# One MoE layer on one core: w2 of the last two expert pairs by column groups in turns, and both pairs' combinations of a group added up in one PSUM bank

## What is computed

```python
h = layer_norm(DEEPNORM_ALPHA * h + mix, ln1_g, ln1_b)
# router: top-1 group of 8, then top-2 of its 4 experts, gates add up to 1
for e in range(32):            # tokens gathered into slots of expert e
    hb = silu(xb @ w1[e]) * (xb @ w3[e])      # w1, w3: 2048 x 512
    y[tokens of e] += gate * (hb @ w2[e])     # w2: 512 x 2048
out = layer_norm(DEEPNORM_ALPHA * h + y, ln2_g, ln2_b)
```

## Time and profile before

| what | us |
|---|---|
| median of 3 runs | 1279.6 |
| lowest and highest | 1278.81 and 1279.9 |
| the profiled execution, its own time | 1281.4 |
| its span, first to last instruction | 1279.6 |
| TensorE busy, share of the span | 1235.5 (97%) |
| VectorE busy | 445.1 (35%) |
| bytes moved, mean rate | 472.28 MB, 369 GB/s |

### The profile page before, as it was taken

One profiled execution on the slowest core, in us unless ns is written; L12 is line 12 of the kernel. 1 busy time (PEld: TensorE's weight loads), 2 busy tenths in 40 slices (PEclk: granted clock), 3 DMA queues, 4 the chain that ended last, 5 costly groups with the idle time before them and its releaser, 6 DMA issues.

```text
span 1279.6 us, 15326 instructions
## 1 busy us (share of the span) xinstructions
PE 1235.5 (97%) x6669; PEld 709.6 (55%) x6669; DVE 445.1 (35%) x635; ACT 319.4 (25%) x545; POOL 7.7 (1%) x17
## 2 busy tenths in 40 slices
PE   6999999999999999999999989899899999989997
PEld 6989989988744444444443444444344444434433
DVE  7889996855310203133130202111010211111026
ACT  5443333533421211111111111111112111111212
POOL 1000000000000000000000000000000000000000
PEclk9999999999999999999999999999999999999998
DMA  9655555696999999999999999999999999999995
GB/s 311 208 187 196 167 195 173 233 370 245 351 393 422 413 411 428 427 426 427 429 431 432 430 430 431 431 430 427 435 425 429 428 426 429 427 427 427 424 406 228
DMA packets 67000, 472.28 MB, mean 369 GB/s; under 512 B 7291, under 2 KB 7875, under 8 KB 41075
## 3 DMA queue, kind: packets, MB, share of 16 engines
q1 hardware_dynamic: 66498, 470.47, 90.4%
q10 hardware_dynamic: 432, 0.79, 0.2%
HBM read 469.14 MB, written 2.10 MB: 368 GB/s over the span
## 4 chain that ended last, share of the span: by engine, by line
PE 82%; DMA 16%; DVE 1%; SPq 0%; issue 0%; ACT 0%; DVEq 0%
PE psum L958 34%; DMA places<-in_w_dram 15%; PE psum L706 9%; PE psum L733 9%; PE psum L1003 8%; PE psum L880 7%; PE psum L662 5%; PE psum L916 2%; PE psum L665 2%; PE psum L917 2%; PE psum L1038 1%; PE psum L945 1%; DMA places<-in_ln_in_b_dram 1%; PE psum L853 1%; DVE area_b L2035 0%; PE psum L627 0%
## 5 line engine op out<-in xcount | busy, mean ns | idle before, releaser
L958 PE MATMUL psum<-places,area_c 128*64 128x512 f32 x2048 | 458.2, 600 | 20.1 <-DMA places<-in_w_dram 20.1
L958 PEld LDWEIGHTS psum<-places,area_c 128*64 128x64 f32 x2048 | 146.6, 138 | 302.7 <-issue 298.4
L1003 PE MATMUL psum<-places,area_d 128*64 128x512 f32 x928 | 204.3, 598 | 2.2 <-DMA places<-in_w_dram 2.2
L1332 ACT ACTIVATE area_c<-psum,gain 128x128 f32<-128x128 f32 x256 | 96.5, 457 | 293.7 <-PE psum L880 293.7
L1905 DVE TENSOR_TENSOR area_a<-area_a,psum 128x512 f32<-128x512 f32 x56 | 38.3, 684 | 355.5 <-PE psum L917 355.5
L1499 DVE TENSOR_TENSOR w_low<-places,w_high 128x2048 fp32r<-128x2048 f32 x55 | 126.0, 2290 | 62.2 <-ACT w_high L1169 62.1
L1169 ACT ACTIVATE w_high<-places 128x2048 fp32r<-128x2048 f32 x55 | 105.4, 1916 | 143.8 <-PE psum L665 42.5
L1003 PEld LDWEIGHTS psum<-places,area_d 128*64 128x64 f32 x928 | 66.3, 138 | 129.5 <-issue 127.4
L880 PE MATMUL psum<-one_hot,area_b 128*128 128x128 f32 x1024 | 124.9, 278 | 0.3 <-DVE one_hot L1831 0.3
L880 PEld LDWEIGHTS psum<-one_hot,area_b 128*128 128x128 f32 x1024 | 118.0, 192 | 12.9 <-issue 12.2
L1889 DVE TENSOR_TENSOR y_low<-psum,y_high 128x512 fp32r<-128x512 f32 x64 | 42.7, 687 | 233.6 <-ACT y_high L1341 233.6
(11 more groups left out here) (220 smaller groups left out, 763.1 us busy)
## 6 DMA issues: line engine op xcount, KB each, us to landing
places<-in_w_dram SPq DMA_DIRECT2D x97, 2048.0 KB, 23.5
places<-in_w_dram SPq DMA_DIRECT2D x27, 4096.0 KB, 21.4
places<-in_w_dram SPq DMA_DIRECT2D x70, 1024.0 KB, 9.7
places<-in_w_in_dram SPq DMA_DIRECT2D x40, 1024.0 KB, 5.1
places<-in_w_out_dram SPq DMA_DIRECT2D x16, 1024.0 KB, 6.5
places<-in_w_dram SPq DMA_DIRECT2D x8, 512.0 KB, 18.5
places<-in_w_dram SPq DMA_DIRECT2D x16, 256.0 KB, 9.3
area_a<-in_x_dram SPq DMA_DIRECT2D x4, 512.0 KB, 6.0
```

The costliest lines, as they stand in the source:

```text
L958: mm = pe.matmul(psum[i * CAP:(i + 1) * CAP, j // UNITS, :], gathered[:, kk, i * CAP:(i + 1) * CAP], w[i][:, k, :], start=kk == 0, stop=kk ...
L1003: mm = pe.matmul(psum[i * CAP:(i + 1) * CAP, 4 + c, :], hidden_t[:, f, i * CAP:(i + 1) * CAP], w[i][:, c, :], start=f == 0, stop=f == FT - 1)
L1332: ins = act.activation(gathered[:, k, :], psum[:, 2 + g % 2, k % 4 * P:(k % 4 + 1) * P], ACT.Identity, scale=gain[:, 0, k:k + 1], bias=gai ...
```

## The change

In steps 14 and 15 the order of the work becomes: w1, w3 of step 14, the turn, w1, w3 of step 15, then w2 of both steps by column groups in turns: step 14 left (c = 0, 1), step 15 left, step 14 right (c = 2, 3), step 15 third (c = 2), step 15 fourth (c = 3). All these products are `column_products(s, f, c, ...)` (s = 0 for step 14, 1 for step 15). Step 14 writes PSUM banks 4 and 5, step 15 banks 6 and 7. There are eight results n = 0 to 7 in the order 14 c0, 14 c1, 15 c0, 15 c1, 14 c2, 14 c3, 15 c2, 15 c3, and eight combinations `combine_last(n)`: that of step 14 starts the bank pair of its group, that of step 15 adds on top, and VectorE adds the sum of both once (`add_last`). The identity matmuls that bring `area_a` into the last group's banks stand in `combine_last(5)`, ahead of the fourth products.

The loads follow: 176 to 183 are w1 and w3 of step 15 as whole halves; 184 and 185 are w2 left of step 14, 186 and 187 left of step 15, 188 and 189 right of step 14 (24 pieces of 512 KB in all), 190 and 191 third and fourth of step 15 (16 pieces of 256 KB). Quarters are used for loads 168 to 171 instead of 182 to 187. From load 132 on, two loads are issued together when the later one of their two slots is free. The rows of the last LayerNorm go to a slot that nothing else uses by then, and wait for nothing.

```diff
@@ last_two_steps, on TensorE
-                unit_products(b, b % TWO, lambda j: arrived(start + 2 * UNITS + j), False, units=range(UNITS))
+                for j in range(2 * UNITS):
+                    unit_products(b, b % TWO, lambda j: arrived(start + 2 * UNITS + j), False, units=(j,))
+                    if j == UNITS:
+                        pe.wait_ge(silu_ready, PAIRS)
...
                 for f in range(FT):
-                    hidden_rows(f, arrived(start + 3 * UNITS + f))
...
+                    for c in range(2):
+                        column_products(0, f, c, [half[:, f, c, :] for half in left], s_left)
+                    if f == FT // 2 - 1:
...
+                        pe.wait_ge(half_hidden, 1)
+                        pe.wait_ge(gt_drained, PAIRS)
...
                 pe.wait_ge(half_kept, 1)
...
+                pe.wait_ge(ht_drained, PAIRS)
+                pe.wait_ge(y_drained, NC * a)
                 for f in range(FT):
...
+                        column_products(1, f, c, [half[:, f, c, :] for half in last_left], s_last_left)
+                    if f < 2:
+                        combine_last(f)
+                pe.wait_ge(y_drained, LAST_Y + 2)
                 for f in range(FT):
...
+                    for c in range(2, NC):
+                        column_products(0, f, c, [half[:, f, c - 2, :] for half in right], s_right)
+                    if f < 2:
+                        combine_last(2 + f)
+                pe.wait_ge(y_drained, LAST_Y + 4)
+                for f in range(FT):
+                    column_products(1, f, 2, [third[:, i, f, :] for i in range(2)], s_third)
+                    if f % 2 == 1:
+                        combine_last(4 + f // 2)
+                for f in range(FT):
+                    column_products(1, f, 3, [fourth[:, i, f, :] for i in range(2)], s_tail)
                     if f == 1:
...
+                        combine_last(6)
+                combine_last(7)
@@ combine_last
+                if s == 0 and c >= 1:
+                    pe.wait_ge(comb_added, LAST_Y + (2 * (c - 1) if c > 1 else 0))
+                if s == 0 and last:
...
                         pe.matmul(psum[:, 2 + t, :], ident[:], area_a[:, t, LAST_COLS], start=True, stop=False)
...
+                    pe.matmul(psum[:, bank, :], by[:, t, :], y_high[:, n % 2, :],
+                              start=s == 0 and not last, stop=False)
+                    mm = pe.matmul(psum[:, bank, :], by[:, t, :], y_low[:, n % 2, :], start=False, stop=s == 1)
@@ the DMA queue
-            for m in range(WHOLE.stop, LAST):
-                load_half(m)
+            for m in range(WHOLE.stop, BY_COLUMNS, 2):
+                unit_used((m + 1 - PLACES) // STEP_UNITS, (m + 1 - PLACES) % STEP_UNITS)
+                if m in (LATE, LATE + 2):
+                    load_pair(m, m - LATE, PAIRS - 2)
...
-            sp.wait_ge(y_ready, NC * (PAIRS - 1))
...
+            last_unit_used(SLOTS - 2)
```

More of the change, by code:

```diff
@@ L918, in combine, with combine_last @@
                 mm.then_inc(comb_ready, 1)
[L920 to L925, removed]
+            def combine_last(n):
+                s, c = n // 2 % 2, n // 4 * 2 + n % 2
                 last = c == NC - 1
-                if last:
+                if s == 0 and c >= 1:
+                    pe.wait_ge(comb_added, LAST_Y + (2 * (c - 1) if c > 1 else 0))
+                if s == 0 and last:
                     for t in range(TT):
                         pe.matmul(psum[:, 2 + t, :], ident[:], area_a[:, t, LAST_COLS], start=True, stop=False)
-                pe.wait_ge(y_drained, NC * it + c + 1)
+                pe.wait_ge(y_drained, LAST_Y + n + 1)
+                by = (one_hot_t, one_hot_t_2)[s]
                 for t in range(TT):
                     bank = 2 * (c % 2) + t
-                    pe.matmul(psum[:, bank, :], one_hot_t_2[:, t, :], y_high[:, c % 2, :], start=not last, stop=False)
-                    mm = pe.matmul(psum[:, bank, :], one_hot_t_2[:, t, :], y_low[:, c % 2, :], start=False, stop=True)
-                    if last and t == 0:
+                    pe.matmul(psum[:, bank, :], by[:, t, :], y_high[:, n % 2, :],
+                              start=s == 0 and not last, stop=False)
+                    mm = pe.matmul(psum[:, bank, :], by[:, t, :], y_low[:, n % 2, :], start=False, stop=s == 1)
+                    if s == 1 and last and t == 0:
                         mm.then_inc(tile0_combined, 1)
@@ L1061, in last_two_steps @@
[L1061 to L1072, removed]
@@ new lines, in pair_of @@
+                def pair_of(m, form, **parts):
+                    return [slots[slot_of(BY_COLUMNS + m + i)].rearrange(form, **parts) for i in range(2)]
+                left, last_left, right = (pair_of(2 * j, "p (f c d) -> p f c d", f=FT, c=2) for j in range(3))
+                third, fourth = pair_of(6, "p (i f d) -> p i f d", i=2, f=FT)
+                for f in range(FT):
+                    for c in range(2):
[3 more added lines that the diff above has]
+                        pe.wait_ge(gt_drained, PAIRS)
+                        for h in range(FT // 2):
+                            mm = pe.transpose(psum[:, 0, h * P:(h + 1) * P], hidden[:, h * P:(h + 1) * P], ident[:])
+                        mm.then_inc(half_turned, 1)
+                        pe.wait_ge(hidden_ready, PAIRS)
+                        for h in range(FT // 2):
+                            at = (FT // 2 + h) * P
+                            mm = pe.transpose(psum[:, 1, h * P:(h + 1) * P], hidden[:, at:at + P], ident[:])
+                        mm.then_inc(ht_ready, 1)
@@ L1087, in last_two_steps @@
                     for c in range(2):
-                        last_rows(f, c, [wide[i][:, f, c, :] for i in range(2)], s_wide)
-                pe.wait_ge(y_drained, NC * b)
+                        column_products(1, f, c, [half[:, f, c, :] for half in last_left], s_last_left)
+                    if f < 2:
+                        combine_last(f)
+                pe.wait_ge(y_drained, LAST_Y + 2)
                 for f in range(FT):
-                    last_rows(f, 2, [narrow[0][:, i, f, :] for i in range(2)], s_third)
-                    if f == 1:
-                        combine_apart(b, 0)
@@ L1395, in last_step @@
                                ACT.Copy).then_inc(ht_drained, 1)
-                for c in range(NC):
-                    keep_y_high(it, c, True)
+                for n in range(2 * NC):
+                    keep_y_high(it - 1, n)
             act.wait_ge(s_gain, 16 * 2)
```

141 lines of the change are left out of this document (56 added, 85 removed).

## The result

The changed kernel takes a median of 1281.84 us (1280.47 to 1285.29, 20 runs), the kernel before 1280.07 us (1278.81 to 1281.86, 20 runs). The ratio is 1.0014, with a 95% interval of 1.0008 to 1.002. That is 1.8 us more, less than the 2.56 us that the prediction's bound of 0.2% allows: no change by that bound, but a small slowing that is clear of the noise, since the interval leaves out 1, and close to the 1281.3 us forecast. The profiled execution took 1282.77 us, with a span of 1281.0 us against 1279.6 before.

The account below looks back on a forecast made before the run. The weight stream bounds the kernel up to 1219.6 us, TensorE from there on. Last product + 2.05, tail - 0.4, so + 1.65 us on the median of 1279.6: 1281.3 forecast, small terms leaving 1280.3 to 1282.4, full range 1279.0 to 1284.0.

Parts of the forecast that it names:

- Landing of load 183: Last half of step 15's w3 lands at 1219.55 us, 0.15 of it added for more loads in quarters.
- the cover named in the prediction: Even loads 132 to 167 issue some 10 us later; two to three loads still queued, so cost nothing.
- Idle time: TensorE idles about 2 us, from 1217.5 to 1219.6, ahead of the last w3 pair.
- TensorE's work from there: From 1219.6 to the last product TensorE has 45.9 us of work, ending at 1265.5.
- Identity matmuls as the main loss: Now ahead of the last product, they make 1.9 of its 2.05 us delay.
- Data in time: After load 183, w2 pieces land at least 1.1 us before use; 2.55 us per 512 KB pair, 1.31 per 256 KB.
- Tail: From last product to tile 0's first statistics: 2.0 us against 2.42 before, 0.4 won.
- Sum: Last product 2.05 us later less 0.4 in the tail: 1.65 us more on the span.
- The clock falls: Rival: the idle time before the last w3 pair drops TensorE's clock, price 1.7 us, 1283.0; chance 0.20.
- Slow pieces: Rival: w2 pieces at 374 GB/s land the last right group row 2.0 us late, 1283.3; chance 0.10.
- TensorE keeps up: Rival: TensorE 4 us quicker than summed, so the end follows the last weight piece, 1277.3; chance 0.07.
- No wait at load 183: Rival: the stream runs 2 us ahead, so TensorE goes on at 1217.5, 1279.3; chance 0.07.

Follow-up runs that it names:

- e1: Changed kernel with the two identity matmuls put back behind the last product: median 1280.82 us, ratio 1.0006 to the kernel before.
- e4: Changed kernel with the identity matmuls done twice in their new place, the second overwriting the first: 1284.09 us, ratio 1.0032 to the kernel before.
- e5: Changed kernel without loading the fourth column group (2 MB); its products read the third group's weights: 1282.56 us, ratio 1.0018 to the kernel before.
- e8: Changed kernel with four unused 128x256 matmuls (1.9 us) in TensorE's idle place ahead of the last w3 pair: 1282.92 us, ratio 1.0024.
- e8b: Same kernel as e8, run again beside the unaltered changed kernel (c1): 1282.57 us, ratio 1.0017 to the kernel before.
- e9: Changed kernel with nine unused matmuls (4.1 us) in the idle place ahead of the last w3 pair: 1284.75 us, ratio 1.0035.
- c1: The changed kernel unaltered, as control: 1281.85 us, ratio 1.0015 to the kernel before.
- e2: Changed kernel with loads 180 to 183 cut into quarters instead of 168 to 171: 1281.37 us, ratio 1.0007 to the kernel before.
- e6: Kernel before with only its identity matmuls moved ahead of the third group's combination: 1281.61 us, ratio 1.0012.
- e3: Changed kernel with the edits of e1 and e2 together: 1280.3 us, ratio 1.0003 to the kernel before.
- e7: e3 with combinations 2 and 3, and 4 and 5, side by side: 1280.31 us, ratio 0.9999 to the kernel before.

## Why the prediction was right

Point by point, by its own steps.

- **Landing of load 183.** Forecast 1219.55, measured 1218.96, 0.6 us early. In the seven other profiles that leave these loads as they are (e1, e4, e5, e8, e8b, e9, c1) it landed between 1216.74 and 1218.99, so how near one execution comes is partly luck, and a term as small as the 0.15 for more quarters can't be seen. The later issues of the even loads cost nothing that shows: the DMA share is 1.00 to 1.01 at 426 to 427 GB/s from 960 to 1210, as the cover named in the prediction wanted.
- **Idle time.** Forecast about 2 us, measured 1.86, 2.04, 1.80 and 1.86 in the changed kernel, e1, e5 and c1, and 1.21 in e4. The mechanism was right, and e2 shows that it is the landing of the last halves that makes it. The term was sized from one profiled execution; in the median execution it may be nearer to 1 us (e8b, e9), which the noise leaves open.
- **TensorE's work from there.** Forecast 45.9 us, measured 45.94, and term by term no further off than 0.15 us: the w3 pair took 7.09 instead of 6.98 and the transposes of `hidden` 0.59 instead of 0.45, while the two row groups ahead of them took 3.43 instead of 3.58. With the earlier landing the last product ends at 1265.04 instead of 1265.5.
- **Identity matmuls as the main loss.** 1.9 of the 2.05 us. Removed (e1), doubled (e4) and added alone (e6), they moved the median by - 1.0, + 2.25 and + 1.5 us. In the two profiles the last product moved by 1.60 us (1263.44 to 1265.04), less than the 1.91 us of these matmuls, so the rest of the new order is even or slightly better there. Of the few tenths that combinations standing singly were to add no run speaks by itself; e1 without them has a ratio of 1.0006 (0.9997 to 1.0015), not told apart from the kernel before.
- **Data in time.** Forecast twelve pairs of 2.55 us; measured (1249.66 - 1218.96) / 12 = 2.56. The last weights landed at 1261.5 instead of 1260.6: here the step was 0.9 us short, since eight pairs took 11.85 us, 1.48 each instead of 1.31. The first six kept to 1.31 (the sixth landed at 1247.9 + 9.6 = 1257.5); the last two took 4.0 us together. The last pair's four records start near 1264.1, half-way through the last eight, so 2.6 us were left, and the miss stayed without effect.
- **Tail.** Forecast 2.0 us, measured 2.17: 1.40 us until y_low is done and read, where 1.35 had been set, and 0.74 for the two matmuls instead of 0.66, since the first took 0.50 behind an idle time.
- **Sum.** + 1.65 us forecast; on the span it was + 1.4 (1281.0), in the medians + 1.8. Two small errors of the trace steps, the landing (0.6 early) and the tail (0.17 long), are opposite in sign. That the median fell within 0.6 us of the forecast says no more than that: the medians' own difference is known to some 0.8 us.

One reading of the kernel before was slightly off: its chain doesn't stay on TensorE all the way from 1239.2, but spends 0.39 us on a copy by ScalarE (L1392) at 1245.21. Nothing in the forecast hangs on it.

The rivals. *The clock falls* did not come to pass: no granted clock of 0.50 between 1219 and 1265 in any of the profiles. But its condition, an idle time somewhat over 2.0 us, was wrong: the last section has a fall behind 1.95 us and none behind 3.05 us. That the clock stayed up behind 1.86 us is therefore not explained by the length of the idle time, and the prediction was in part lucky there. *Slow pieces*: no wait on a piece in the changed kernel. The Trainium skill's page "DMA: Bandwidth & Descriptors", section Bandwidth, measures 341 GB/s for a DMA of 1 MB and less for smaller ones. The trace disagrees as it did before: 403 GB/s over the 30.8 us of the 24 pieces of 512 KB, a pair of 1.05 MB each 2.56 us, and no wait. *TensorE keeps up* is false here, since TensorE waited for no piece and finished 3.5 us behind the last weights (1265.04 against 1261.5); in e3, the nearest to it, this was 1.7 us (1261.28 against 1259.6). *No wait at load 183* is false in both profiles of the changed kernel; whether the wait is shorter in the median execution stays open.

## What to carry to other kernels

Work that doesn't depend on the last data can be cheapest behind the last product, when the copying that follows leaves its engine idle there anyway: 1.9 us of matmuls cost 0.25 us in that place, and 1.7 us ahead of the last product (e1, e4). Before an order is refined to follow a stream more finely, see which of the two is bound at that point: from load 183 on 45.9 us of TensorE's work stood against 42.5 us of loads, and e5 took 2 MB of them away for no gain. A gap in front of a late load was 1.2 to 2.0 us long in five profiles of this study, so one profile doesn't size it; filling it with work of two lengths, with enough runs, does so better.

## What the runs showed of the hardware

- The length of an idle time doesn't tell whether TensorE's clock falls behind it. The first three rows below stand at the same place of the program, the first pair of w3 units of step 14. In the changed kernel TensorE stood idle for 2.07 us, and the granted clock fell to 0.50, the 1.2 GHz level, so that 32 records took 8.78 us; in e4 it fell behind 1.95 us. In c1, which is the changed kernel again, it stayed at 1.00 behind 3.05 us, and 32 records took 7.09. The earlier trace rows had 2.24 with a fall and 2.01 without one, and e1 had 2.04 without one ahead of 1218.39. What decides it, the runs don't show. The fall at 1170 cost nothing that shows, since the stream was the bound there.

```profile
1169.17 8.78 PE L957 MATMUL psum<-places,area_c 128*64 128x512 f32 x32 [2.07 <-DMA places<-in_w_dram]
```

The same view of e4, of c1, and of e1 at its later place:

```profile
1167.58 8.79 PE L958 MATMUL psum<-places,area_c 128*64 128x512 f32 x32 [1.95 <-DMA places<-in_w_dram]
```

```profile
1169.15 7.09 PE L957 MATMUL psum<-places,area_c 128*64 128x512 f32 x32 [3.05 <-DMA places<-in_w_dram]
```

```profile
1218.39 7.09 PE L957 MATMUL psum<-places,area_c 128*64 128x512 f32 x32 [2.04 <-DMA places<-in_w_dram]
```

- A wait is put down to what came last, and that can be another engine's work: 0.6 us at the same place in e2, e3 and e7 were named `y_low`, on which the instruction doesn't depend.
- Pieces of 256 KB for the last two groups took 1.48 us a pair on average here and 1.31 us before. The difference lies in the last two of the eight pairs, 4.0 us together; what slowed them was not tried.
